# Seven block products instead of eight in 36 gate/up pairs of a two-block network, the weight sums made by GpSimd

## The reference

```python
        h = rms_norm(x, norm_ffn_w[i])
        g = jnp.einsum("bld,df->blf", h, w_gate[i])
        u = jnp.einsum("bld,df->blf", h, w_up[i])
        x = x + jnp.einsum("blf,fd->bld", jax.nn.silu(g) * u, w_down[i])

def swiglu_ffn(x, w_in, w_out):
    g, u = jnp.split(x @ w_in, 2, axis=-1)
    return (jax.nn.silu(g) * u) @ w_out
```

## Time and profile before

| | |
|---|---|
| median of 3 runs | 2700.85 us (2699.92 to 2701.69) |
| profiled execution, span | 2697.8 us |
| what lies around the span | 3.05 us, the median less the span; no time but the span is recorded for the profiled execution |
| TensorE busy | 2665.9 us, 99% |
| VectorE busy | 1526.9 us, 57% |
| ScalarE busy | 1173.5 us, 43% |
| GpSimd busy | 26.8 us, 1% |
| 6768 wide matmuls with HHI or HLO | 893.2 + 878.8 + 878.3 us of TensorE's busy time |
| mean granted clock of TensorE | 0.999 of 2.4 GHz |

### The profile page before, as it was taken

How to read it: one execution, slowest core, us unless ns; L and a number is a source line. 1 busy time by engine, 2 the same in 40 slices (tenths; PEclk the granted TensorE clock), 3 DMA queues, 4 the chain that set the end, 5 groups by cost and what they waited for, 6 DMA issues and landing times.

```text
span 2697.8 us, 33846 instructions
## 1 busy us (share of the span) xinstructions
PE 2665.9 (99%) x13860; PEld 2195.1 (81%) x13860; DVE 1526.9 (57%) x2142; ACT 1173.5 (43%) x1732; POOL 26.8 (1%) x45
## 2 busy tenths in 40 slices
PE   9989999999989999999999999999999999999998
PEld 8777888888777888888888888888777888888887
DVE  7885444345885444344444356899978844544433
ACT  6784332225784322233322234455688452432221
POOL 0000000000000000000000000000000000000000
PEclk9999999999999999999999999999999999999999
DMA  6303333324303333333333342222223432333332
GB/s 216 94 2 110 100 96 95 98 83 148 94 2 110 102 94 97 97 94 97 100 94 96 98 138 86 72 74 76 77 86 96 133 94 94 98 98 94 98 94 67
DMA packets 75801, 255.55 MB, mean 95 GB/s; under 512 B 9088, under 2 KB 12288, under 8 KB 75264
## 3 DMA queue, kind: packets, MB, share of 16 engines
q1 hardware_dynamic: 73136, 240.29, 29.3%
q0 software_dynamic: 2512, 13.11, 1.3%
HBM read 241.30 MB, written 8.39 MB: 93 GB/s over the span
## 4 chain that ended last, share of the span: by engine, by line
PE 93%; DVE 4%; ACT 3%; issue 1%; DVEq 0%; ACTq 0%
PE PS L1469 27%; PE PS L1471 27%; PE PS L1470 27%; PE PS L1719 1%; PE PS L1701 1%; PE PS L1428 1%; PE PS L1488 1%; PE PS L1487 1%; PE PS L1489 1%; DVE WLO L2216 0%; PE PS L1665 0%; ACT WHI L1805 0%; PE PS L1537 0%; PE PS L1535 0%; PE PS L1539 0%
## 5 line engine op out<-in xcount | busy, mean ns | idle before, releaser
L1469 PE MATMUL PS<-HHI,WHI 128*128 128x512 f32 x2256 | 893.2, 396 | 0.0
L1471 PE MATMUL PS<-HHI,WLO 128*128 128x512 f32 x2256 | 878.8, 390 | 0.0
L1470 PE MATMUL PS<-HLO,WHI 128*128 128x512 f32 x2256 | 878.3, 389 | 0.0
L2216 DVE TENSOR_TENSOR WLO<-WR,WHI 128x1024 fp32r<-128x1024 f32 (+2 forms) x450 | 535.0, 1191 | 495.4 <-ACT WHI L1805 492.2
L1805 ACT CAST WHI<-WR 128x1024 fp32r<-128x1024 f32 (+2 forms) x450 | 457.5, 1018 | 445.6 <-PE PS L1471 421.9
L1469 PEld LDWEIGHTS PS<-HHI,WHI 128*128 128x128 f32 x2256 | 423.6, 188 | 92.1 <-issue 4.8
L1470 PEld LDWEIGHTS PS<-HLO,WHI 128*128 128x128 f32 x2256 | 423.7, 188 | 89.9 <-issue 4.1
L1471 PEld LDWEIGHTS PS<-HHI,WLO 128*128 128x128 f32 x2256 | 423.4, 188 | 88.8
L1469 PE MATMUL PS<-FHI,WHI 128*128 128x512 f32 x682 | 265.3, 389 | 0.0
L1470 PE MATMUL PS<-FLO,WHI 128*128 128x512 f32 x682 | 265.3, 389 | 0.0
L1471 PE MATMUL PS<-FHI,WLO 128*128 128x512 f32 x682 | 265.3, 389 | 0.0
(11 more groups left out here) (381 smaller groups left out, 2727.5 us busy)
## 6 DMA issues: line engine op xcount, KB each, us to landing
WR<-in_stream SPq DMA_DIRECT2D x402, 512.0 KB, 3.6
WR<-in_stream SPq DMA_DIRECT2D x32, 384.0 KB, 3.0
xkeep<-X POOLq DMA_DIRECT2D x3, 2048.0 KB, 9.4
X<-xkeep POOLq DMA_DIRECT2D x24, 256.0 KB, 4.7
WR<-in_stream SPq DMA_DIRECT2D x16, 328.0 KB, 4.0
ROT<-RQ SPq DMA_DIRECT2D x40, 64.0 KB, 2.0
X<-in_xin SPq DMA_DIRECT2D x8, 256.0 KB, 4.9
out<-X SPq DMA_DIRECT2D x8, 256.0 KB, 2.2
```

The source lines that it names most:

```text
L1469: e.matmul(out, hi[:, i, :], xhi, start=first, stop=False)
L1470: e.matmul(out, hi[:, i, :], xlo, start=False, stop=False)
L1471: t = e.matmul(out, lo[:, i, :], xhi, start=False, stop=final)
L2216: e.tensor_tensor(lo, raw, hi.bitcast(F32), ALU.subtract).then_inc(S["dve_low"], 1)
```

## The change

**Seven for eight.** In the pairs j = 5, 7, ..., 21 of each stage (9 of 22) gate and up weights are seen as a matrix of 2x2 blocks, each of four 128x128 blocks (first or second four rows; gate or up), and the tokens as 2x2 (first or second half of the rows; first or second 256 tokens). Eight block products become seven, by sums of weights and of tokens, in the manner of Strassen and Winograd. A block product is 12 matmuls of 256 columns (lines `srow`). Such a pair holds three banks; `PRODUCTS` gives bank, half and whether it starts afresh. The gate/up pairs between, and 0 to 4, stay as they were ("eight-pairs").

**Token sums.** Four combinations of halves of the scaled tokens are made once a stage, while pairs 0 to 4 run: steps `sv`, `ss`, `sd`, then their rounded parts and remainders `sshi` (SHI) and `sslo` (SLO).

**Weight sums.** Four sums of 128x512 for each seven-pair are made by GpSimd (`tsum`, into WT and WT2) while the eight-pair ahead runs, then rounded in two casts of 1024 on ScalarE (`thi`, THI) and two subtractions of 1024 on VectorE (`tlo`, TLO). Product 1 waits for the second `tlo`. Only half of the up slot needs splitting (`high` and `low` of 512). `tsum` waits for both loads and for the `mul` of the seven-pair before; the reload of a raw slot waits for the sums.

**Combining.** Two copies of PSUM on ScalarE (`snap`: P1 behind product 0, Q5 behind product 2), and on VectorE `dd`, `ww` (two steps), `gs` (two), `cc` (two), then `mul` on SBUF alone. They use the memory of WT and WT2.

**Parts.** Room for SHI, SLO, THI, TLO and WT comes from halving FHI and FLO to 11 rows: the stage runs pairs 0 to 10, then 8 down products of 11 rows, added to X by `padd`, then pairs 11 to 21 and 8 down products of 11 rows. Down slots have 6 and 5 rows instead of 8, 8 and 6. `last_tile` has 11 rows. The main ring of banks has 6 banks in these stages, and `xscale` runs two tiles behind each of the pairs 5 to 8.

The core of the diff:

```diff
+PARTS = (range(0, 11), range(11, 22))
+PART = 11
+DOWN = (((0, 6), (6, 5)), ((11, 6), (17, 5)))
+SEVEN = range(5, FT, 2)
+PRODUCTS = ((0, 0, True), (1, 0, True), (2, 0, True), (0, 1, False), (0, 0, False), (1, 0, False), (2, 0, False))
...
-    "hrow": (("pe", 0.28709),), "hadd": (("dve", 0.48237),), "hsq": (("act", 0.63007),), "hsum": (("pe", 0.51453),),
+    "hrow": (("pe", 0.28709),), "srow": (("pe", 0.36),), "snap": (("act", 0.4),), "dd": (("dve", 0.45),), "ww": (("dve", 1.0),),
...
+            if k - RAW in self.pair_of and not self.summed(self.pair_of[k - RAW]):
+                break
...
+        self.ring.update(main=(0, 1, 2, 3, 4, 5), side=(6, 7))
+        self.spawn(self.combined(f))
+        for part, rows in zip(PARTS, DOWN):
+            for j in part:
+                if j + 1 in SEVEN:
+                    self.spawn(self.weight_sums(f, j + 1))
+                if j in SEVEN:
+                    self.seven(f, gate, up, i, up0, j)
+                else:
+                    self.eight(f, gate, up, i, up0, j)
+                self.add("fhi", f, j)
+                self.add("flo", f, j)
+                if m == 5 and 5 <= j < 5 + DT // 2:
+                    self.run(lambda: ("sd", f) in self.n)
+                    for t in (2 * j - 10, 2 * j - 9):
+                        self.x["xscale", 4, t] = self.x_now[t]
+                        self.x_now[t] = self.add("xscale", 4, t)
...
+    def seven(self, f, gate, up, i, up0, j):
+
+        keys = ("seven", f, j, 0), ("seven", f, j, 1), ("seven", f, j, 2)
+        for key in keys:
+            self.take(key)
+        slots = self.slot(gate, i, 0, j * P), self.slot(up, i, 0, up0 + j * P)
+        self.slot_of["seven", f, j] = slots
+        self.run(lambda: ("tlo", f, j, 1) in self.n)
+        for u in range(7):
+            for r in range(4):
+                self.add("srow", f, j, u, r)
...
+            if u == 0 or u == 2:
+                self.add("snap", f, j, u // 2)
+            elif u == 1:
+                self.add("dd", f, j)
+            elif u == 5:
+                self.add("ww", f, j)
+                self.free(keys[0], ("dve_gs", self.add("gs", f, j)))
+                self.add("silu", f, j)
+        self.free(keys[1], ("dve_gs", ("gs", f, j)))
+        self.free(keys[2], ("dve_gs", self.add("cc", f, j)))
+        self.add("mul", f, j)
...
+    def weight_sums(self, f, j):
+
+        yield from self.added(("sslo", f, 3))
+        last = max(k for k, pair in self.pair_of.items() if pair == (f, j))
+        while last - RAW not in self.low:
+            yield 0.1
+        for i in range(4):
+            yield self.add("tsum", f, j, i)
+        self.advance()
+        for k in range(2):
+            self.add("thi", f, j, k)
+        for k in range(2):
+            yield ("thi", f, j, k)
+            self.add("tlo", f, j, k)
...
+                    elif u == 1:
+                        q.wait_ge(S["dve_xlow"], n["tlo", f, j, 1])
+                        q.wait_ge(S["dve_xlow"], n["sslo", f, 3])
+                    elif u == 3:
+                        q.wait_ge(S["act_uhi"], n["snap", f, j, 0])
+                    elif u == 5:
+                        q.wait_ge(S["dve_gs"], n["dd", f, j])
+                    elif u == 6:
+                        weights_split(q, k_up)
+                        q.wait_ge(S["act_uhi"], n["snap", f, j, 1])
...
+            elif kind == "snap":
+                f, j, k = a
+                q.wait_ge(S["dve_xlow"], n["tlo", f, j, 1])
+                q.wait_ge(S["pe_prod"], o.product_end[f, j, 2 * k])
+                e.copy((P1, Q5)[k], PS[o.bank["seven", f, j, 2 * k]][:, HALVES[0]]).then_inc(S["act_uhi"], 1)
...
+            elif kind == "tsum":
+                f, j, i = a
+                k_gate, k_up = o.slot_of["seven", f, j]
...
+                e.tensor_tensor(WT[i // 2][:, i % 2, :], left, right, ALU.add).then_inc(S["pool_ya"], 1)
```

More of the change, by code:

```diff
@@ L353, in product @@
         self.rhs[p] = rhs
+        self.first[p] = rows[0][0]
         self.take(p)
@@ L506, in ffn @@
         m = NORM_FFN[f]
+        for pair in SEVEN:
+            at_ = self.slots.index((gate, i, 0, DT, pair * P, P))
+            self.pair_of[at_] = self.pair_of[at_ + 1] = (f, pair)
+        self.x["sv", f] = list(self.x_now)
         self.advance(SPL)
@@ L510, in ffn @@
         self.run()
[L511 to L517, removed]
-            self.free(("up", f, j), ("dve_mul", self.add("mul", f, j)))
-            self.add("fhi", f, j)
-            self.add("flo", f, j)
-            if m == 5 and 4 <= j < 4 + DT:
-                self.x["xscale", 4, j - 4] = self.x_now[j - 4]
-                self.x_now[j - 4] = self.add("xscale", 4, j - 4)
@@ L524, in ffn @@
-        for j in range(DT):
-            if (f, j) == (len(NORM_FFN) - 1, DT - 1):
-                self.last_tile(f, down, i, j)
-                continue
-            self.product(("out", ADD_FFN[f], j), ("F", f), down, i, j * P, ((0, 8), (8, 8), (16, 6)))
-            self.add_to_x(ADD_FFN[f], AFTER_NORM[m], j)
+        self.ring.update(main=(0, 1, 2, 3, 4, 5), side=(6, 7))
+        self.spawn(self.combined(f))
+        for part, rows in zip(PARTS, DOWN):
+            for j in part:
+                if j + 1 in SEVEN:
[11 more added lines that the diff above has]
+                        self.x_now[t] = self.add("xscale", 4, t)
+            if part is PARTS[-1]:
+                self.ring.update(main=(0, 1, 2, 3), side=(4, 5, 6, 7))
+            for j in range(DT):
+                if part is not PARTS[-1]:
+                    self.product(("part", f, j), ("F", f), down, i, j * P, rows)
+                    self.x["padd", f, j] = self.x_now[j]
+                    self.x_now[j] = self.add("padd", f, j)
+                    self.free(("part", f, j), ("dve_add", self.x_now[j]))
+                elif (f, j) == (len(NORM_FFN) - 1, DT - 1):
+                    self.last_tile(f, down, i, j)
+                else:
+                    self.product(("out", ADD_FFN[f], j), ("F", f), down, i, j * P, rows)
+                    self.add_to_x(ADD_FFN[f], AFTER_NORM[m], j)
@@ new lines, in combined @@
+    def combined(self, f):
+        yield self.add("sv", f)
+        for k in range(4):
+            if k < 3:
+                done = self.add("ss", f, k)
+            else:
+                done = self.add("sd", f)
+            yield done
+            yield self.add("sshi", f, k)
+            self.add("sslo", f, k)
+    def weight_sums(self, f, j):
[11 more added lines that the diff above has]
+            self.add("tlo", f, j, k)
@@ L544, in last_tile @@
         self.spawn(self.last_half(0))
-        for r in range(FT):
+        for r in PARTS[-1]:
             _, i, nr = self.slot_of[p, r]
@@ L1557, in tensor_engine @@
                 q.wait_ge(S["dve_xlow"], n["flo", o.rhs[p][1], r])
[L1558 to L1560 removed]
+                e.matmul(out[:, part], hi[:, i, :], FHI[:, r % PART, part], start=r == PART, stop=False)
+                e.matmul(out[:, part], hi[:, i, :], FLO[:, r % PART, part], start=False, stop=False)
+                t = e.matmul(out[:, part], lo[:, i, :], FHI[:, r % PART, part], start=False, stop=r == FT - 1)
                 if h == 0 and r == FT - 1:
```

249 lines of the change are left out of this document (219 added, 30 removed).

## The result

| | |
|---|---|
| median before, beside it | 2700.39 us (2699.47 to 2701.69) |
| median after | 2794.31 us (2790.13 to 2794.79, 4 runs) |
| ratio | 1.0345, 95% interval 1.0331 to 1.0360 |
| profiled execution, span | 2792.5 us, before 2697.8 |
| mean granted clock of TensorE | 0.983, before 0.999 |

The account below looks back on a forecast made before the run. TensorE, busy for 2665.9 of 2697.8 us, was taken as the bound, any new wait paid in full. Terms -28.8 + 61.6 + 2.7 + 15.2 + 3.5 = +54.2 gave span 2752.0, time 2755 us; range 2735 to 2792.

Parts of the forecast that it names:

- matmuls of 36 pairs: TensorE, gate/up stages: 48 wide steps become 84 narrow ones, saving 0.80 us a pair, 28.8 us in all.
- second TLO: Product 1 waits for VectorE's second TLO behind multiply and FLO: 2.2 us a pair, 61.6 us for 28 pairs.
- pairs 7 and 9 of norm 5: Two multiply-adds of X also stand ahead of the second TLO on VectorE: +2.7 us.
- first pairs of a stage: Token-sum work delays the first TLO in each stage's first seven-pair: stall 3.8 us, 15.2 us for four stages.
- fall of the clock: Rival: TensorE's clock falls in each stall, 1.7 us a pair, 54 us more, 2809 us; chance 0.07.
- split and last tile: Down products' split hidden, 0 us; last tile 4.0 us shorter, earlier part 7.5 us longer: +3.5 us.
- weight sums, table loads, combining: GpSimd's sums, ScalarE's function table loads, VectorE's combining steps: each taken as hidden, 0 us.
- the pace of issue: TensorE's steps: 0.2267 us for 512 columns, 0.120 us for 256, so a narrow matmul costs 53% of a wide one.
- rival of the hidden wait: Product 0 and queue slack cover the second TLO, leaving only -28.8 and +3.5: 2675.6 us; chance 0.06.
- high sum of 2786: +85 us: 5.5 us for first pairs, 0.5 more for each other, 1.7 for each of six stalls over 3.3 us.
- rival of the late sums: GpSimd's weight sums, pushed by VectorE, delay THI, FHI and TLO: 28 us more, 2783, or 78 more, 2833; chance 0.08.

Follow-up runs that it names:

- e4: Only the 11-row parts, six-bank ring, moved rescaling and shorter last tile, all 88 pairs eight-pairs, against the kernel before: 2704.39 us, ratio 1.0017.
- e1: Changed kernel with both TLO remainders on VectorE ahead of the eight-pair's multiply: 2702.94 us, ratio 1.0005 to the kernel before.
- e2: Changed kernel without ScalarE's function table loads at step `dd` and again at silu, order unchanged: 2793.55 us, ratio 1.0339 to the kernel before.
- e3: Changed kernel with 14 more narrow matmuls between product 0 and product 1's wait, result overwritten: 2774.63 us, ratio 1.0273 to the kernel before.
- e10: Changed kernel with 7 more narrow matmuls between product 0 and product 1's wait, result overwritten: 2772.93 us, ratio 1.0268 to the kernel before.
- e5: As e1, with norm 5's rescaling of X moved behind eight-pairs 6, 8 and 10: 2693.41 us, ratio 0.9973 to the kernel before.
- e6: Changed kernel with the four weight sums a pair on VectorE instead of GpSimd, same order: 2788.28 us, ratio 1.0327 to the kernel before.
- e7: As e4, with the last tile's second-half add ahead of the first half's eight scalings on VectorE: 2700.87 us, ratio 1.0004 to the kernel before.
- e8: e1, e5, e2 and e7 together, with pair 5 of norm 5's stage left an eight-pair: 2681.05 us, ratio 0.9929 to the kernel before.
- e9: As e8, with the four weight sums a pair on VectorE, same order: 2680.95 us, ratio 0.9928 to the kernel before.

## Why the prediction was right or wrong, step by step

| term | forecast | measured |
|---|---|---|
| matmuls of 36 pairs | -28.8 | -28.8: the four pairs 11 last 10.08 us |
| second TLO, 26 normal pairs behind the first of a stage | 57.2 (2.2 each) | 58.5 (2.25 each) |
| pairs 7 and 9 of norm 5 | 7.1 (3.55 each) | 13.5 (6.74 each) |
| first pairs of a stage | 15.2 (3.8 each) | 6.8 for three (2.25 each) and 8.0 |
| fall of the clock | 0, a rival at 0.07 | 22.5 in 15 normal pairs, 7.4 in three long ones |
| split and last tile | 3.5 | 3.5 (e4) |
| weight sums, table loads, combining | 0 | 0 but for norm 5 (e1, e2) |
| sum | 54.2 | 91.4; the spans differ by 94.7 |

Of the 37.2 us that the sum missed 29.9 are the clock's and 7.3 lie in the stalls themselves, nearly all in pairs 7 and 9 of norm 5. Without the clock's part the time would have lain inside the range.

**What bounds the kernel, and the pace of issue**: right. 84 narrow steps took 10.08 us wherever nothing was waited for. The Trainium skill, "TensorE: Matmul & The Clock Gate", section "Back-to-back issue gap", gives 262 cycles for 256 columns and 518 for 512. By these figures the change would save an estimated 1.19 us a pair; the traces show 0.80.

**The second remainder**: right in its cause, place, number and size. The multiply was forecast 0.27 us, FLO 1.64 and the second TLO 2.25 us behind the first step of the pair; in pair 7 they come at 0.55, 1.91 and 2.52, and in pair 9 TensorE stood for 2.03 us. e1 shows the cause by removing it. The rival of the hidden wait fell, for the reason given: the queue is in order.

**The falling clock**: this is the step that failed, by 30 of the 37 us that the sum missed. The prediction put the clock at zero in the sum and took it as a rival that comes in all stalls or in none, with 0.07, since before the change it fell only 2 to 3 us behind TensorE's last matmul; only the high sum of 2786 had it, in the six longest stalls. A pause of 2.1 us lies at the lower edge of just that, and "not by much" would have had to become a part of the sum: it fell in half of the pauses. That it could fall when TensorE was at work again, up to 1.7 us behind the restart, was not thought of. The price of a fall was near: 1.7 us was said, 1.5 us came, and 2.1 to 2.7 us behind the long pauses. The 3.4 us for which a fall would last stood on no row of before; behind the ordinary stalls it lasted 2.6 to 3.4 us. e3 and e10 show the part that the clock has: with the pause filled and the wait left, 20 us go. The Trainium skill, "TensorE: Matmul & The Clock Gate", section "What's actually happening", says that activity releases the clock and idleness throttles it; the traces agree, with a clock of 0.66 in the window around the pause and no fall in twice 29 pauses shortened by matmuls whose result is thrown away.

**The first pairs of a stage**: mis-sized both ways. The last remainder of the token sums was put so late that it would push the first TLO. In the stages of norms 1, 3 and 7 it was early enough: GpSimd started its sums at 298.92, 9.1 us ahead of pair 5, and the stall was the ordinary one. In the stage of norm 5 VectorE's work begins later: the `gs` of pair 0, which needs the row scale, starts 19.5 us behind that pair's first step (1275.79 against 1256.33), in the stage of norm 1 13.3 us (266.08 against 252.76). That this is why the token sums end late is likely, and no run tests it. The sums of GpSimd started at 1310.26 and ended at 1316.76 for a pair begun at 1312.04; the cast into THI, and behind it FHI, FLO and TLO, came after them. It is the rival of the late sums, in one pair out of 36. That the four first pairs together came to 14.8 us against 15.2 is luck: three were far shorter and one twice as long.

**Pairs 7 and 9 of norm 5**: right that two rescaling steps stand ahead of the second TLO (1.41 us, 1348.65), wrong that this is all. Two more of them stand behind the seven-pair's FLO, beside GpSimd's sums, and cost 3.47 us there. The prediction had noted the pushes of VectorE and GpSimd, and had given them slack in a normal pair, where they cost nothing, but did not add them up in this stage, where VectorE has four more steps in every two pairs. e5 shows that the place of these steps is worth the whole stall that e1 had left in the two pairs, 3.4 us each, with the clock's part behind it; how much of it is the neighbour's, e5 and e6 don't tell.

**The sums of GpSimd** were put at 1.1 us from the earlier trace rows; they took 1.48 on average. Four of them are 1.5 us longer, more than the 1.2 us of slack that had been counted, and yet in 27 of the 29 normal pairs nothing was late, and in the other two the stall was 0.3 us longer. With the stall gone (e1) both remainders are ready within 0.3 us of the time at which they are wanted: most pairs last 10.33 and not 10.07 us.

**Last tile, parts, table loads, combining**: right, the first three by e4 and e2, the combining since TensorE waits at no other place inside a seven-pair than in front of product 1. The 3.5 us can be had back by the place of one add (e7). 3.3 us of the difference of the spans are in none of these terms and stay open; single executions of the changed kernel differ by up to 4.7.

## What to carry to other kernels

When a chain of small steps feeds the next product through an in-order queue, ask for each of its instructions what stands ahead of it and what releases that: here one instruction queued behind a step that waits for the end of the running product turned 29 us of gain into a loss of 94, and moving it was worth 91. Price a pause of the matrix engine as the pause plus the clock: a pause of about 2 us between dense matmuls cost 2.25 us, and half of the time 1.5 us more. Work given to idle GpSimd is not free for VectorE: steps beside it took up to 1.77 us instead of 0.69, so compare it with doing it on VectorE (e8 and e9 came out equal).

## What the runs showed of the hardware

The clock of TensorE fell in 15 of 29 pauses of some 2.1 us, all between stretches of dense matmuls, in as many in e2 and in e6, and in none of 58 pauses of 0.25 to 1.45 us (e3, e10). It fell up to 1.7 us after TensorE had started again. After a fall 12 to 16 narrow steps took 0.213 us instead of 0.120, behind the three long pauses of the changed kernel 20 to 26.

GpSimd and VectorE hold each other up, but not always. Both at once, in the first stage of the changed kernel:

```profile
300.29 1.62 POOL L2978 TENSOR_TENSOR WT<-WT,WR 128x512 f32<-128x512 f32 x1
301.99 1.62 POOL L2978 TENSOR_TENSOR WT<-WR 128x512 f32<-128x512 f32 x1
...
300.68 1.77 DVE L2418 TENSOR_TENSOR WLO<-WR,WHI 128x512 fp32r<-128x512 f32 x1
302.82 0.69 DVE L2553 TENSOR_TENSOR SQF<-PS,RS 128x512 f32<-128x512 f32 x1 [0.37 <-PE PS L1609]
```

The subtraction of two tiles of SBUF took 1.77 us instead of 0.69, while the multiply with one input in PSUM ran inside a sum of GpSimd and took its usual 0.69 us. The Trainium skill, "SBUF — State Buffer", section "SBUF: two separate sides", names exactly this case for the shared port, a VectorE instruction with two SBUF inputs against a GpSimd one that reads SBUF; the trace agrees in both halves. GpSimd's own sums differ too: the shortest of the 144 took 1.26 us, the middle one 1.61, the longest 2.16.
